# Sums of squares in the gated delta layer: one float32 product against two rounded products of a square split by GpSimd

## What is computed

```python
def gdn_mixer(h, w_in, w_conv, a_log, dt_bias, w_onorm, w_out):
    proj = h @ w_in
    ...
    qkv = jax.nn.silu(causal_conv(qkv, w_conv))
    q, k, v = jnp.split(qkv, 3, axis=-1)
    ...
    q = q * lax.rsqrt(jnp.sum(q * q, axis=-1, keepdims=True) + EPS) * (1.0 / math.sqrt(d))
    k = k * lax.rsqrt(jnp.sum(k * k, axis=-1, keepdims=True) + EPS)
    ...
    o = chunk_gated_delta(q, k, v, g, beta)
    o = o * lax.rsqrt(jnp.mean(o * o, axis=-1, keepdims=True) + EPS) * w_onorm.astype(jnp.float32)
    ...
    return (o * jax.nn.silu(z)) @ w_out
```

## Time and profile before

| | before |
|---|---|
| median of 3 runs | 2028.37 us |
| lowest and highest | 2026.86 and 2028.68 us |
| span of the profiled execution, first to last instruction | 2026.0 us |
| median less that span | 2.4 us |
| PE busy | 2000.9 us, 99% of the span |
| DVE busy | 1455.5 us, 72% |
| ACT busy | 584.3 us, 29% |
| POOL busy | 353.2 us, 17% |

### The profile page before, as it was taken

The page is one execution under the profiler, slowest core; times in us unless marked ns, Lnnn a source line. Parts: engine busy times, 40 slices in busy tenths (PEclk is TensorE's granted clock), DMA queues, the critical chain, the costliest instruction groups (busy, mean ns, idle before and its releaser), DMA issues.

```text
span 2026.0 us, 31822 instructions
## 1 busy us (share of the span) xinstructions
PE 2000.9 (99%) x12918; PEld 1608.2 (79%) x12918; DVE 1455.5 (72%) x2281; ACT 584.3 (29%) x1013; POOL 353.2 (17%) x317
## 2 busy tenths in 40 slices
PE   9999999999999999999999999999999999999999
PEld 7888888887777777777888877777888888888887
DVE  6666666667867777678997877576566769849973
ACT  2000122222655454434873233533210010000000
POOL 2121111111110110011112212111112212222221
PEclk9999999999999999999999999999999999999999
DMA  5323322222211121122222323111223323322232
GB/s 184 102 90 99 100 84 78 94 84 75 85 64 54 64 70 58 65 84 84 63 73 84 126 78 99 42 63 48 78 83 94 107 91 104 104 94 94 94 99 89
DMA packets 53361, 173.52 MB, mean 86 GB/s; under 512 B 6464, under 2 KB 6720, under 8 KB 53088
## 3 DMA queue, kind: packets, MB, share of 16 engines
q1 hardware_dynamic: 48112, 161.46, 24.2%
q10 hardware_dynamic: 5104, 10.03, 1.9%
HBM read 169.30 MB, written 2.16 MB: 85 GB/s over the span
## 4 chain that ended last, share of the span: by engine, by line
PE 85%; DVE 9%; ACT 4%; issue 2%; DMA 1%; ACTq 0%; DVEq 0%; SPq 0%
PE ps_lin L1934 24%; PE ps_lin L1936 23%; PE ps_lin L1935 23%; PE ps_att L1983 7%; PE ps_aux L1983 4%; DVE arena L436 3%; ACT arena L1362 2%; DVE arena L430 2%; PE ps_att L1992 1%; DVE w_lo L430 1%; ACT L1368 1%; DVE arena L433 1%; PE ps_lin L1954 1%; PE ps_lin L1956 0%; PE ps_lin L1955 0%
## 5 line engine op out<-in xcount | busy, mean ns | idle before, releaser
L1934 PE MATMUL ps_lin<-xw_hi,w_hi 128*128 128x512 f32 x1704 | 689.9, 405 | 1.2 <-issue 0.6
L1936 PE MATMUL ps_lin<-xw_hi,w_lo 128*128 128x512 f32 x1704 | 665.6, 391 | 0.0
L1935 PE MATMUL ps_lin<-xw_lo,w_hi 128*128 128x512 f32 x1704 | 664.8, 390 | 0.0
L412 POOL TENSOR_SCALAR w_hi<-raw 128x1024 fp32r<-128x1024 f32 (+2 forms) x309 | 348.8, 1129 | 1655.3 <-PE ps_lin L1936 1537.3
L1362 ACT ACTIVATE arena<-arena 128x512 f32<-128x512 f32 (+7 forms) x331 | 206.4, 630 | 750.2 <-DVE arena L430 361.4
L430 DVE TENSOR_TENSOR w_lo<-raw,w_hi 128x1024 fp32r<-128x1024 f32 (+2 forms) x340 | 376.6, 1110 | 45.5 <-POOL w_hi L412 16.9
L1934 PEld LDWEIGHTS ps_lin<-xw_hi,w_hi 128*128 128x128 f32 x1704 | 320.6, 188 | 68.5 <-issue 4.3
L1936 PEld LDWEIGHTS ps_lin<-xw_hi,w_lo 128*128 128x128 f32 x1704 | 320.1, 188 | 68.6
L1935 PEld LDWEIGHTS ps_lin<-xw_lo,w_hi 128*128 128x128 f32 x1704 | 320.9, 188 | 59.3 <-issue 0.5
L430 DVE TENSOR_TENSOR arena<-ps_lin,rstd 128x512 f32<-128x512 f32 (+3 forms) x220 | 147.6, 671 | 182.4 <-PE ps_lin L1936 173.9
L1934 PE MATMUL ps_lin<-y_hi,w_hi 128*128 128x512 f32 (+1 forms) x544 | 205.2, 377 | 0.0
(11 more groups left out here) (188 smaller groups left out, 1697.2 us busy)
## 6 DMA issues: line engine op xcount, KB each, us to landing
raw<-in_w_up SPq DMA_DIRECT2D x44, 512.0 KB, 3.3
raw<-in_conv_w_in SPq DMA_DIRECT2D x32, 512.0 KB, 3.3
raw<-in_fox_w_in SPq DMA_DIRECT2D x32, 512.0 KB, 3.3
raw<-in_gdn_w_in SPq DMA_DIRECT2D x32, 512.0 KB, 3.3
raw<-in_w_gate SPq DMA_DIRECT2D x24, 512.0 KB, 3.3
raw<-in_swa_w_in SPq DMA_DIRECT2D x20, 512.0 KB, 3.3
raw<-in_w_ml SPq DMA_DIRECT2D x16, 512.0 KB, 4.0
raw<-in_w_down SPq DMA_DIRECT2D x16, 512.0 KB, 3.5
```

The costliest lines, as they stand in the source:

```text
L412: pool.tensor_scalar(w_whole(n, kc * c)[0], w_raw(n, kc * c), 1.0, 0.0, mult, add).then_inc(s("w_rounded"), 1)
L1934: pe.matmul(o, wh, hi, start=first and k == 0, stop=False)
L1935: pe.matmul(o, wh, lo, start=False, stop=False)
L1936: ins = pe.matmul(o, wl, hi, start=False, stop=last and k == kc - 1)
```

## The change

The 24 sums are made from two parts. ACT squares twice: once into `sq` in float32 as before, and once more, from the same source, into `y_hi` in float32r, which rounds. POOL subtracts the rounded square from the full one into `y_lo`, also float32r. PE adds two float32r products of 512 columns with a float32r matrix of ones (or of 1/128), the high part first. The matrix `sum_w` is written once by POOL at the start.

The semaphores `gdn_sq` and `gdn_osq` now follow the second square, and PE waits for `gdn_low`, which POOL raises. POOL's subtractions have fixed places among its rounding of weights: that of a query or key stands behind the rounding of the unit three after the tile's own, that of an output behind the rounding of the unit three after z of the head that is being projected. In PE's order the sums of query and key stand one chunk later than before, and that of an output two chunks later. To free a semaphore, DVE's `gdn_kd` is counted on `gdn_vb`; its waits mean the same as before.

```diff
+        LOW_QK = {LAST_UNIT[tile_of("gdn_w_in", part * GDN_H + r)] + 3 for r in range(GDN_H) for part in range(2)}
+        LOW_O = {LAST_UNIT[tile_of("gdn_w_in", 3 * GDN_H + r)] + 3: r - 1 for r in range(1, GDN_H)}
+        LOW_O[LAST_UNIT[tile_of("gdn_w_out", BANKS)]] = GDN_H - 1
...
-        FIRST_SQUARES = {2 * ND + 2: 1, 3 * ND + 1: 2}
+        FIRST_SQUARES = {2 * ND + 3: 1, 3 * ND + 2: 2}
...
+                if n in LOW_O:
+                    h = LOW_O[n]
+                    pool.wait_ge(s("gdn_osq"), h + 1)
+                    pool.tensor_tensor(y_lo[:, h, :], sq[:, 0, :], y_hi[:, h, :].bitcast(f32), sub).then_inc(s("gdn_low"), 1)
+                if n in LOW_QK:
+                    qk_low += 1
+                    pool.wait_ge(s("gdn_sq"), qk_low)
+                    pool.tensor_tensor(y_lo[:, GDN_H - 1, :], sq[:, 1, :], y_hi[:, GDN_H - 1, :].bitcast(f32), sub).then_inc(s("gdn_low"), 1)
...
-                    activation(sq[:, 1, :], dst, ACT.Square).then_inc(s("gdn_sq"), 1)
+                    activation(sq[:, 1, :], dst, ACT.Square)
+                    activation(y_hi[:, GDN_H - 1, :], dst, ACT.Square).then_inc(s("gdn_sq"), 1)
...
-                activation(sq[:, 0, :], ps_att[:, 0, :], ACT.Square).then_inc(s("gdn_osq"), 1)
+                activation(sq[:, 0, :], ps_att[:, 0, :], ACT.Square)
+                activation(y_hi[:, h, :], ps_att[:, 0, :], ACT.Square).then_inc(s("gdn_osq"), 1)
...
-                    pe.wait_ge(s("gdn_sq"), 2 * r + part)
+                    pe.wait_ge(s("mean_set"), 3)
+                    pe.wait_ge(s("gdn_low"), LOW_COUNT["qk", 2 * r + part])
                     pe.wait_ge(*aux("gdn_rn", 2 * r + part))
-                    mm_last(ps_aux[:], mat("ones"), sq[:, 1, :]).then_inc(s("gdn_ss"), 1)
+                    mm(ps_aux[:], sum_w[:, 0, :], y_hi[:, GDN_H - 1, :], True, False)
+                    mm(ps_aux[:], sum_w[:, 0, :], y_lo[:, GDN_H - 1, :], False, True).then_inc(s("gdn_ss"), 1)
...
+                fill(2)
                 if h:
                     gdn_squares(h - 1)
-                fill(GDN_FILL["squares"])
+                fill(GDN_FILL["squares"] - 2)
...
-                pe.wait_ge(s("gdn_osq"), h + 1)
-                mm_last(ps_aux[:], mat("mean_h"), sq[:, 0, :]).then_inc(s("gdn_oss"), 1)
+                pe.wait_ge(s("gdn_low"), LOW_COUNT["o", h])
+                mm(ps_aux[:], sum_w[:, 1, :], y_hi[:, h, :], True, False)
+                mm(ps_aux[:], sum_w[:, 1, :], y_lo[:, h, :], False, True).then_inc(s("gdn_oss"), 1)
...
-                            if r and done[0] % ND == ND - 1:
-                                gdn_tile(r, done[0] // ND)
+                            if r and done[0] and done[0] % ND == 0:
+                                gdn_tile(r, done[0] // ND - 1)
```

More of the change, by code:

```diff
@@ L304, in block_program @@
         swa["sin"] = rstd_final[:]
+        sum_w = sb("sum_w", [P, 2, P], f32r)
         gate_norm = {"fox_w_f": cols[:, ND:2 * ND], "gdn_w_gates": cols[:, 2 * ND:3 * ND], "ml_w_gates": mix_w[:]}
@@ L363, in block_program @@
         NORM_COL = [("norm_w", 0), ("norm_w", ND), ("norm_w", 2 * ND), ("norm_w", 3 * ND), ("g_mix_2", 0), ("g_ffn_2", 0)]
+        LOW_QK = {LAST_UNIT[tile_of("gdn_w_in", part * GDN_H + r)] + 3 for r in range(GDN_H) for part in range(2)}
+        LOW_O = {LAST_UNIT[tile_of("gdn_w_in", 3 * GDN_H + r)] + 3: r - 1 for r in range(1, GDN_H)}
+        LOW_O[LAST_UNIT[tile_of("gdn_w_out", BANKS)]] = GDN_H - 1
+        LOW_COUNT = {}
+        for n in sorted(LOW_QK | set(LOW_O)):
+            if n in LOW_O:
+                LOW_COUNT["o", LOW_O[n]] = len(LOW_COUNT) + 1
+            if n in LOW_QK:
+                LOW_COUNT["qk", sum(("qk", i) in LOW_COUNT for i in range(2 * GDN_H + 1)) + 1] = len(LOW_COUNT) + 1
         X_IN = [("x_in0", 16), ("x_in1", 16), ("x_in2", 32), ("x_in2", 32), ("x_in3", 32), ("x_in3", 32), ("x_in4", 32), ("x_in4", 32)]
@@ L399, in _ @@
             pool.memset(v_tmp[:, 0:P], 1.0 / D).then_inc(s("mean_set"), 1)
+            pool.memset(sum_w[:, 0, :].bitcast(f32), 1.0).then_inc(s("mean_set"), 1)
+            pool.memset(sum_w[:, 1, :].bitcast(f32), 1.0 / P).then_inc(s("mean_set"), 1)
+            qk_low = 0
             for n, (w, i, k0, kc, c, _, _, _, _, t) in enumerate(UNITS):
@@ L802, in gdn_head @@
                 step(tt(chunks(F["kbg"]), chunks(ps_att[:, 1, :]), column(1, h), mult))
-                tt(chunks(F["kd"]), chunks(ps_att[:, 1, :]), column(2, h), mult).then_inc(s("gdn_kd"), 1)
+                tt(chunks(F["kd"]), chunks(ps_att[:, 1, :]), column(2, h), mult).then_inc(s("gdn_vb"), 1)
                 dve.wait_ge(s("gdn_tok"), 2 * h + 2)
                 tt(chunks(F["vb"]), chunks(ps_att[:, 2, :]), column(0, h), mult).then_inc(s("gdn_vb"), 1)
-                dve.wait_ge(s("gdn_vb"), h + 1)
+                dve.wait_ge(s("gdn_vb"), 2 * h + 2)
                 if 0 < h < GDN_H - 1:
@@ L2144, in gdn_head @@
                 four(X, lambda c: blk(k_, c), B("kb")).then_inc(s("gdn_A"), 1)
-                pe.wait_ge(s("gdn_kd"), h + 1)
+                pe.wait_ge(s("gdn_vb"), 2 * h + 1)
                 four(Y, lambda c: blk(k_, c), lambda c: blk(q_, c)).then_inc(s("gdn_A"), 1)
                 fill(GDN_FILL["U0"])
-                pe.wait_ge(s("gdn_vb"), h + 1)
+                pe.wait_ge(s("gdn_vb"), 2 * h + 2)
                 fill(1)
```

## The result

| | before | after |
|---|---|---|
| median | 2028.09 us | 2042.05 us |
| lowest and highest | 2026.86 and 2028.68 us | 2040.51 and 2043.48 us |
| ratio, with 95% interval | | 1.0072 (1.0060 to 1.0084) |
| span of the profiled execution | 2026.0 us | 2039.6 us |

The changed kernel is 14 us slower (four runs of each). The forecast was slower by 6.7, 2035.1, with a range of 2024 to 2040; the sign was right, the size was half of it, and the range too low.

What follows compares the result with a forecast made beforehand. PE was busy 99%, but its waits for other engines were taken to decide. Terms 2.2 - 0.8 + 1.2 + 2.4 + 0.8 + 0.95 = +6.75 us gave 2028.4 + 6.7 = 2035.1 us, range 2024 to 2040.

Steps and rivals of the forecast that it cites:

- the size of the subtraction: Duration of each of POOL's 24 subtractions: 1.05 us taken, between 0.62 and 1.24.
- The price that I put on a duration: In DVE's back-to-back work, a POOL operation of 1.05 us costs DVE 0.84 us, one of 0.62 costs 0.41.
- the output's place: Output's sum, heads 2 to 7: POOL's subtraction delays DVE's gate and PE's `four(X)`, +0.37 us each, +2.2 over six.
- With 0.62 for the operation: Rival, POOL quick or finding DVE's gaps: terms at their lower ends nearly cancel, +0.9 us, 2029.3; chance 0.27.
- half a collision at the key: Key's sum: POOL before DVE's `w_lo` half makes PE 0.40 us later, otherwise nothing; half taken, 0.20, +1.2 over six heads.
- The query: Query's sum, seven heads: PE waits 0.31 of the 0.42 us saved, behind ACT's delayed copy; -0.11 each, -0.8 in all.
- The key's saving of 0.42 that does not count: Key's sum: PE's saved 0.42 us is lost, since PE already waits for DVE's copy after the convolution steps.
- An ordinary head: One repeated head with the output's +0.37, the query's -0.11 and the key's +0.20 us.
- The first head: First head's two sums: longer chain of squares and subtractions, and DVE held up in its convolution steps; +2.4 us (1.2 to 3.4).
- The last head: Last head: one more POOL operation delays DVE's `w_lo`, for which PE already waits; +0.8 us (0.4 to 1.0).
- Behind it: Behind the last head: the chain from ACT's square to Ln gets longer and binds; +0.95 us (0.5 to 1.1).
- the slow rival: POOL's subtraction lasts 2 us, so the query's sum also waits and output and key lose more; 2042 us, chance 0.06.

Runs made afterwards that it cites:

- the filler run: The changed kernel plus 26 products with unused results, placed where its PE stands (first head, last sum); 2039.37 us, ratio 1.0060 against the kernel before.
- the three sums made as before: Changed kernel with the first head's two sums and last output's sum as before, the other 21 at later places; 2023.05 us, ratio 0.9976 against before.
- the quicker operation: The changed kernel with POOL rounding the square itself (one operand, 512 columns) instead of subtracting; 2029.67 us, ratio 1.0012 against the kernel before.

## Why the prediction was right in sign and wrong in size

**The mechanism held.** The pair of `w_lo` halves, `four(X)` behind the gate, the query's second group 0.06 behind ACT's copy, PE standing before the first head's sums and the last one: all of it is in the profile after, and the runs without the subtraction and with it moved take it away again.

**The first step that failed: the size of the subtraction.** I put it between 0.62 and 1.24 us and took 1.05, the duration of a rounding that reads as many elements. It takes 1.26 to 1.29 where nothing holds it up, beyond my upper end. The estimate of 1.11 before dispatch, drawn from the page "GPSIMD Engine Reference" of the Trainium skill, section "Elementwise — side-by-side cycle accounting", was nearer; the trace gives 0.15 to 0.18 on top of it. I named it and left it out of the sum. The price that I put on a duration was right: 0.84 for 1.05 is the duration less 0.21, which would make 1.06 of 1.27. DVE's loss is 1.10 instead of 0.84, and PE starts 0.14 behind the gate where I had 0.05, so the output's place costs 0.73 per head and not 0.37. With 0.62 for the operation the prediction's sum gave 2029.3, and the run with such an operation 2029.67; that they are so close is partly luck, since it was +0.9 foretold against +2.6 measured, from a lower start on that chip.

**The second: half a collision at the key.** I took the two orders as equally likely, 0.20 a head. POOL was first in all six heads, by 0.05 to 0.06 us in five of them, and with the larger operation the price is 0.64 a head. A margin of 0.1 us between two fixed orders of events came out the same way each time; it was not a matter of halves.

**The third: the clock.** No term of the sum had it. In the first head and behind the last, PE stood and then ran at the lower clock from 536.1 to 539.5 and from 887.7 to 891.1. It cost 1.2 to 1.4 there and 0.85 here, 2.1 to 2.3 in all. For the first head the filler run bears out that PE's standing brought it; behind the last head the same stop left the clock full in two runs, so what brought it there is not shown.

**The rest, point by point.**

- The query: -0.11 foretold. Between `four(X)` and the third level the head lost 0.73, then 0.83, then 0.63, so the query gave back 0.20.
- The key's saving of 0.42 that does not count: right. Without the subtraction the lead over before, in heads that no stop disturbs, is 0.47 us ahead of the key's sum (26.52 against 26.99 behind z), 0.87 behind it (29.62 against 30.49), and 0.47 again at the copy before the scan,'s place (34.63 against 35.10).
- An ordinary head: 0.73 + 0.10 - 0.20 + 0.64 = 1.27, from 43.0 to 44.27, where I had 0.46. Six times it would be 7.6; the trace shows 6.4. The difference lies in the kernel before, where three of the heads had a stop of PE of 0.5 to 0.6 us (at 641.16, 685.06 and 728.93), two in the middle of a group of small products and one right behind such a group, and were 0.6 to 0.8 longer for it; the changed kernel has two others, of 0.3 (602.74 and 827.17). Such waits of PE ahead of small products in the delta layer of the kernel before, the two at 641.16 and 685.06 among them (waited for: us, times, longest):

```profile
PE ps_att L1983 <- issue: 1.7, 4, 0.6
```

- The first head: 2.4 foretold; 4.1 measured, of which 1.2 to 1.4 is the clock and the rest the waits. DVE's three steps take 3.91 instead of 2.33, +1.58, near the two times 0.84 that I had.
- The last head: +0.8 foretold; from the seventh mark to the last square it is 37.21 instead of 36.30, +0.9.
- Behind it: +0.95 foretold; the chain has +1.40. The subtraction has 0.21 of the difference, and the hand-overs to POOL, PE and ACT, for which I had 0.2 in all, most of the rest. The clock adds 0.85.
- Nothing else was lost: the terms above give 4.1 + 6.4 + 3.1 = 13.6.

**The range.** The upper ends of all terms gave +10.5 where +13.6 was measured, and four of them were passed: the output's sums 4.4 for 3.4, the keys' 3.8 for 2.4, the first head 4.1 for 3.4, and behind the last head 2.25, with the clock, for 1.1. The range left out the slow rival, which had 0.06. That rival's point, an operation clearly longer than 1.05, was the true one, though with 1.27 and not 2 us; that its 2042 is the measured time is luck, since the query's wait in it did not come.

## What to carry to other kernels

An operation given to POOL costs DVE nearly its own length (1.10 of 1.27 us, 0.42 of 0.62) wherever DVE works back to back on operands in SBUF, so the question is not how much POOL is idle but what DVE does at the moment when the input is ready. A wait that delays POOL until DVE reads PSUM can cost nothing and give the loss back (11.7 us here, the rest of the 18 coming from the three sums made as before), provided that the consumer is moved behind it too. Price a new operation by the form it has, not by the nearest one with as many elements, and where a change makes PE stand several times in a short stretch, allow for slower products after it.

## What the runs showed of the hardware

- A waiting POOL operation gets in between two DVE instructions that stand back to back; DVE then loses 1.10 us to an operation of 1.27 and 0.42 to one of 0.62. The page "SBUF — State Buffer" of the Trainium skill, section "SBUF: two separate sides", says that between GpSimd and a VectorE instruction with two inputs in SBUF the shared port pair is an exclusive lock for the whole instruction; the rows agree. Beside DVE's reads of PSUM the subtraction took 1.29 and DVE lost nothing.
- The lower clock did not come after every stop. In the first head it came after stops of 1.0, 1.1 and 2.1 us within 15 us (the changed kernel, and the later subtraction of output or key), and after 0.36, 0.44 and 2.08 (the quicker operation), but not without the subtraction, where one stop of 2.4 us was left. Behind the last head the same stop of 1.9 us was followed by the lower clock in two profiles (the changed kernel, and the first head's sums as before) and by the full clock in two others (the later subtraction of output or key). What decides there stays open.
- The clock also differs between executions of one kernel, and the time with it. Of fifteen executions of the kernel before (on the chip of the filler run), the four with a mean granted clock of 1.000 took 2025.9 to 2026.2 us, and the two with 0.998 took 2030.2 and 2030.8. In the profiles, the part from the last `ps_att<-mats,sq` product on PE to the end takes 953.9 us with no stretch at the lower clock near 1190 us (the first head's sums as before), 955.3 to 955.5 with one, and 956.7 with one of twice the length (the two later subtractions).
- PE has short stops, put down to "issue", inside or right behind groups of small products, in other heads in each kernel. They make heads of the same program differ by up to 0.9 us. They do not fall just anywhere: counted through PE's records in order of time (matmuls, weight loads and those of its sequencer), all 23 such stops above 0.2 us between 540 and 880 us come at a record whose number leaves 194 or 195 when it is divided by 256, in all seven profiles that have any (8386, 9666 and 10946 for the three of the kernel before). Most places of that kind show no stop; the profiles of the later output's subtraction and of the quicker operation show none at all. What PE waits for there, and why only at some of these places, is not shown.
